# Mixed MLA and forgetting attention, convolution and recurrent blocks on one core: the probabilities of the MLA heads are scaled on GpSimd, with five smaller moves between engines

## The reference, cut to what matters

```python
q = (rms_norm(c_q, g_cq) @ w_uq).reshape(b, l, MLA_HEADS, MLA_QK)
q = rope_tail(rms_norm(q, g_q_mla), cos, sin)
...
s = jnp.einsum('bqhd,bkhd->bhqk', q_blk, k) * scale
s = jnp.where(mask[None, None], s, NEG)
p = jax.nn.softmax(s, axis=-1)
return jnp.einsum('bhqk,bkhd->bqhd', p.astype(v.dtype), v)
```

```python
log_a = LRU_C * r * jax.nn.log_sigmoid(lam)
a = jnp.exp(log_a)
mult = jnp.sqrt(-jnp.expm1(2.0 * log_a))
bterm = mult * (i * xb)
_, hs = lax.associative_scan(_lin_rec_op, (a, bterm), axis=1)
y = hs * g
return y @ w_out
```

## Time and profile before

| | before |
|---|---|
| median of three runs | 1333.24 us (1332.63 to 1337.25) |
| the profiled execution, own time | 1332.28 us |
| its span, first to last instruction | 1330.5 us |
| PE busy | 1302.3 us, 98% |
| DVE busy | 953.9 us, 72% |
| ACT busy | 743.5 us, 56% |
| POOL busy | 342.7 us, 26% |
| mean granted TensorE clock | 0.996 of full speed |

### The profile page before, as it was taken

One profiled execution on the slowest core, in us unless ns is written; L12 is line 12 of the kernel. 1 busy time (PEld: TensorE's weight loads), 2 busy tenths in 40 slices (PEclk: granted clock), 3 DMA queues, 4 the chain that ended last, 5 costly groups with the idle time before them and its releaser, 6 DMA issues. The chain is left out here.

```text
span 1330.5 us, 28216 instructions
## 1 busy us (share of the span) xinstructions
PE 1302.3 (98%) x10550; PEld 1274.0 (96%) x10550; DVE 953.9 (72%) x1426; ACT 743.5 (56%) x1192; POOL 342.7 (26%) x374
## 2 busy tenths in 40 slices
PE   9998999999999999999999999999999989999997
PEld 8987899999999999999899999999999989999996
DVE  6867787655487776655455669998559898999844
ACT  5555554444343554444556556666457886666542
POOL 4632133310011233200006214343103022434311
PEclk9999999999999999999999999999999999999998
DMA  9520155555555455555545545554564445555451
GB/s 307 187 100 1 67 188 190 189 191 180 174 185 188 159 190 189 190 187 177 205 158 186 190 155 199 188 182 147 186 214 173 169 167 198 205 183 180 158 191 55
DMA packets 35370, 230.50 MB, mean 173 GB/s; under 512 B 4062, under 2 KB 5214, under 8 KB 11910
## 3 DMA queue, kind: packets, MB, share of 16 engines
q1 hardware_dynamic: 34228, 226.99, 48.6%
q10 hardware_dynamic: 1058, 2.38, 0.5%
HBM read 228.17 MB, written 1.05 MB: 172 GB/s over the span
## 5 line engine op out<-in xcount | busy, mean ns | idle before, releaser
L392 DVE TENSOR_TENSOR wlo<-raw,whi 128x1024 fp32r<-128x1024 f32 (+1 forms) x446 | 525.5, 1182 | 104.7 <-ACT whi L386 102.2
L427 PE MATMUL ps<-xhi,whi 128*128 128x256 f32 (+2 forms) x1920 | 542.9, 283 | 4.9 <-DVE wlo L392 3.9
L428 PE MATMUL ps<-xlo,whi 128*128 128x256 f32 (+2 forms) x1920 | 542.0, 282 | 0.0
L429 PE MATMUL ps<-xhi,wlo 128*128 128x256 f32 (+2 forms) x1920 | 540.8, 282 | 0.0
L386 ACT ACTIVATE whi<-raw 128x1024 fp32r<-128x1024 f32 (+2 forms) x444 | 446.8, 1011 | 153.3 <-PE ps L429 135.7
L427 PEld LDWEIGHTS ps<-xhi,whi 128*128 128x128 f32 x1920 | 362.4, 189 | 8.6 <-issue 5.6
L429 PEld LDWEIGHTS ps<-xhi,wlo 128*128 128x128 f32 x1920 | 362.9, 189 | 0.0
L428 PEld LDWEIGHTS ps<-xlo,whi 128*128 128x128 f32 x1920 | 360.7, 188 | 0.3
L427 PE MATMUL ps<-hhi,whi 128*128 128x256 f32 (+1 forms) x1184 | 334.3, 282 | 2.0 <-issue 0.8
L429 PE MATMUL ps<-hhi,wlo 128*128 128x256 f32 (+1 forms) x1184 | 333.2, 281 | 0.0
L428 PE MATMUL ps<-hlo,whi 128*128 128x256 f32 (+1 forms) x1184 | 333.0, 281 | 0.0
(11 more groups left out here) (339 smaller groups left out, 1338.1 us busy)
## 6 DMA issues: line engine op xcount, KB each, us to landing
raw<-w SPq DMA_DIRECT2D x182, 1024.0 KB, 4.9
raw<-w SPq DMA_DIRECT2D x40, 768.0 KB, 4.2
raw<-w SPq DMA_DIRECT2D x4, 512.0 KB, 5.4
h<-x_fm ACTq DMA_DIRECT2D x4, 272.0 KB, 5.6
out_fm<-h SPq DMA_DIRECT2D x6, 128.0 KB, 1.9
ws<-ws_src ACTq DMA_DIRECT2D x1, 512.0 KB, 3.5
bs<-bs_rows ACTq DMA_DIRECT2D x1, 512.0 KB, 5.0
consts<-constants SPq DMA_DIRECT2D x1, 508.0 KB, 10.4
```

What stands on the lines that cost most here:

```text
L392: nc.vector.tensor_tensor(wlo[:, w, 0:n], raw[:, slot, col:col + n], whi[:, w, 0:n].bitcast(F32), ALU.subtract).then_inc(wlo_done, 3 if fr ...
L427: nc.tensor.matmul(o, hi, xh, start=start, stop=False)
L428: nc.tensor.matmul(o, hi, xl, start=False, stop=False)
L429: mm = nc.tensor.matmul(o, lo, xh, start=False, stop=stop)
```

## The change

Six edits. (1) The two scalings in `normal` are left to POOL for the eight MLA heads; item 9 and the fox heads stay on DVE, and so does the reciprocal. (2) The power -1/2 of the query sums moves from ACT (Ln, Exp) to DVE, as a shift, a subtraction and two Newton steps, eight instructions of 128x24, in step 7 ahead of the last `k_normed`; the sums themselves are made one step earlier (`q_stats` parts 2 and 3 both in `turn(3)`). (3) `key_spread` stands behind `turn` and `values` of its step in place of ahead of them. (4) Of the log-sigmoid of `lam` only the first two instructions stay where they were; the other 15 move behind `dve_mlp_up` of the first MLP. (5) In mixer B the products of scan and gate for pairs 0, 2 and 4 move from DVE to POOL, and POOL does them before its L2334 and L2337. (6) The rounding of these three products (`B_HIGH`) moves from ACT to DVE, directly ahead of the subtraction.

```diff
@@ -18,6 +18,7 @@
 F32R = mybir.dt.float32r
+I32 = mybir.dt.int32
 ACT = mybir.ActivationFunctionType
@@ -1154,9 +1155,9 @@
                     pe.wait_ge(freed, n)
-                if 1 <= j < 6:
-                    q_stats(j - 1)
-                if j == 6:
+                for part in {1: (0,), 2: (1,), 3: (2, 3), 4: (4,)}.get(j, ()):
+                    q_stats(part)
+                if j == 5:
                     pe.wait_ge(s("q_stats_out"), 2)
@@ -1234,12 +1235,12 @@
                     scores(st)
-                if st in KEY_SPREAD:
-                    key_spread(KEY_SPREAD[st])
                 if st < NIT + 2:
                     turn(st - 2)
                 if items[st - 3][0] == "h":
                     values(items[st - 3][1])
+                if st in KEY_SPREAD:
+                    key_spread(KEY_SPREAD[st])
                 if st >= NIT:
@@ -1458,6 +1459,24 @@
+            def query_power():
+
+                c, y, z, mean = s("q_power"), q_inv[:, :, :], q_neg[:, :, :], q_part[:, 0:3, :]
+                yi = y.bitcast(I32)
+                dve.wait_ge(s("q_mean"), 1)
+                nc.vector.tensor_scalar(yi, mean.bitcast(I32), 1, None, ALU.logical_shift_right).then_inc(c, 1)
+                dve.wait_ge(c, 1)
+                nc.vector.tensor_scalar(yi, yi, -1, 0x5F3759DF, ALU.mult, ALU.add).then_inc(c, 1)
+                for k in range(2):
+                    dve.wait_ge(c, 3 * k + 2)
+                    nc.vector.tensor_tensor(z, y, y, ALU.mult).then_inc(c, 1)
+                    dve.wait_ge(c, 3 * k + 3)
+                    nc.vector.scalar_tensor_tensor(out=z, in0=z, scalar=-0.5, in1=mean, op0=ALU.mult,
+                                                   op1=ALU.mult).then_inc(c, 1)
+                    dve.wait_ge(c, 3 * k + 4)
+                    nc.vector.scalar_tensor_tensor(out=y, in0=z, scalar=1.5, in1=y, op0=ALU.add,
+                                                   op1=ALU.mult).then_inc(c, 1)
+
             def peak(j):
@@ -1485,6 +1504,8 @@
                 nc.vector.reciprocal(sf[:, 3, :], sf[:, 2, :]).then_inc(rc_done, 1)
+                if j > D1:
+                    return
                 dve.wait_ge(rc_done, j + 1)
@@ -1508,6 +1529,8 @@
                     normal(st - 1)
+                if st == 7:
+                    query_power()
                 if st in KEY_FINAL:
@@ -1605,16 +1628,18 @@
             dve.wait_ge(s("params_loaded"), 16)
-            for _ in dve_log_sigmoid(dve, par("lam", 0, NB), half_lam[:, :], tmp[:, 0, 0:NB], tmp[:, 1, 0:NB],
-                            tmp[:, 0, NB:2 * NB], s("lam_step"), s("lam_exp_asked"), s("lam_exp")):
+            lam = dve_log_sigmoid(dve, par("lam", 0, NB), half_lam[:, :], tmp[:, 0, 0:NB], tmp[:, 1, 0:NB],
+                            tmp[:, 0, NB:2 * NB], s("lam_step"), s("lam_exp_asked"), s("lam_exp"))
+            next(lam)
+
+            dve_residual(dve, ph["attn_out"], 1, 1, C1, T1)
+            dve_rstd(dve, 1, C1, T1, ph["mlp0_up"])
+            dve_mlp_up(dve, ph["mlp0_up"], C1, T1)
+            for _ in lam:
                 pass
             nc.vector.tensor_scalar(half_lam[:, :], tmp[:, 0, NB:2 * NB], 4.0, None, ALU.mult).then_inc(s("lam_done"), 1)
             nc.vector.tensor_scalar(par("b_b_a", 0, 2 * NB), par("b_b_a", 0, 2 * NB), 0.5, None,
                                     ALU.mult).then_inc(s("gate_bias_done"), 1)
-
-            dve_residual(dve, ph["attn_out"], 1, 1, C1, T1)
-            dve_rstd(dve, 1, C1, T1, ph["mlp0_up"])
-            dve_mlp_up(dve, ph["mlp0_up"], C1, T1)
             dve_residual(dve, ph["mlp0_down"], 4, 2, C1, T1)
@@ -1714,6 +1739,9 @@
             def low_b(m):
+                if m < 6:
+                    dve.wait_ge(u_done, hid0["b_in"] + m + 2)
+                    nc.vector.tensor_copy(hhi2[:, m:m + 2, :], xb[:, m:m + 2, :]).then_inc(uhi_done, 2)
                 dve.wait_ge(uhi_done, hid0["b_in"] + m + 2)
@@ -1763,8 +1791,9 @@
                                                  ALU.add).then_inc(s("b_scan"), 1)
-                if k in B_MULT:
+                if k in B_MULT and B_MULT[k] >= 6:
                     m = B_MULT[k]
+                    dve.wait_ge(u_done, hid0["b_in"] + m)
                     dve.wait_ge(s("b_scan"), m + 2)
@@ -1828,13 +1857,6 @@
-            def query_power():
-
-                act.wait_ge(s("q_mean"), 1)
-                nc.scalar.activation(q_neg[:, :, :], q_part[:, 0:3, :], ACT.Ln).then_inc(s("q_log"), 1)
-                act.wait_ge(s("q_log"), 1)
-                nc.scalar.activation(q_inv[:, :, :], q_neg[:, :, :], ACT.Exp, scale=-0.5).then_inc(s("q_power"), 1)
-
             def roots(n):
@@ -1902,7 +1924,7 @@
                                          ACT.Copy).then_inc(pt0_done, 1)
-                if j == 5:
+                if j == 4:
                     nc.scalar.activation(q_part[:, :, :], ps[:, 6, 2 * P:2 * P + 4 * HEADS].rearrange(
@@ -1924,8 +1946,6 @@
                     turned(st - 2)
-                if st == 7:
-                    query_power()
                 if st >= 3 and second(st - 3) and items[st - 3][1] < HEADS:
@@ -2109,8 +2129,9 @@
                     nc.scalar.activation(hhi2[:, t, :], xb[:, t, :], ACT.Copy).then_inc(uhi_done, 1)
-                if k in B_HIGH:
+                if k in B_HIGH and B_HIGH[k] >= 6:
                     t = B_HIGH[k]
+                    act.wait_ge(uhi_done, hid0["b_in"] + t)
                     act.wait_ge(u_done, hid0["b_in"] + t + 2)
@@ -2269,7 +2290,7 @@
             c, scale, y, z = q_scale, QK ** -0.5, q_inv[:, :, :], q_neg[:, :, :]
-            pool.wait_ge(s("q_power"), 1)
+            pool.wait_ge(s("q_power"), 8)
             nc.gpsimd.tensor_tensor(z, y, y, ALU.mult).then_inc(c, 1)
@@ -2282,8 +2303,19 @@
             nc.gpsimd.tensor_scalar(z, y, -1.0, None, ALU.mult).then_inc(c, 1)
-            pool.wait_ge(pt0_done, early_turned(D1 + 1))
+            pool.wait_ge(pn_done, parts_done(D1 + 1))
             for i in range(HEADS, NHD):
+                if i % 2 == 0:
+                    if i > HEADS:
+                        pool.wait_ge(d_done, i)
+                    for j in (item_of[i], item_of[i + 1]):
+                        pool.wait_ge(rc_done, j + 1)
+                        for k, (n, a, z) in enumerate(parts(j)):
+                            pr = prob_of(j)[0:n, a:z]
+                            nc.gpsimd.tensor_scalar(pr, pr, soft[0:n, j % 2, 3, k:k + 1], None, ALU.mult).then_inc(pn_done, 1)
+                    pool.wait_ge(pn_done, parts_done(item_of[i + 1] + 1))
+                if i == HEADS:
+                    pool.wait_ge(pt0_done, early_turned(D1 + 1))
                 hd, r = heads[i][4], slice(2 * META * (i % 2), 2 * META * (i % 2) + META)
@@ -2329,6 +2361,11 @@
                                             ALU.subtract).then_inc(ulo_done, 1)
+            for m in (0, 2, 4):
+                pool.wait_ge(s("b_scan"), m + 2)
+                pool.wait_ge(s("b_gelu"), m + 2)
+                nc.gpsimd.tensor_tensor(xb[:, m:m + 2, :], work1[:, m:m + 2, :], h_gates(m, 2),
+                                        ALU.mult).then_inc(u_done, 2)
             for m in (6, 8):
                 pool.wait_ge(s("b_aa"), m + 2)
                 nc.gpsimd.tensor_scalar(square_b(m), square_b(m), 1.0, None, ALU.add).then_inc(s("b_plus"), 1)
```

## The result

| | before | changed |
|---|---|---|
| median | 1332.99 us (6 runs, 1331.82 to 1337.25) | 1339.73 us (6 runs, 1337.98 to 1341.37) |
| ratio, 95% interval | | 1.0046 (1.0034 to 1.0058) |
| the profiled execution, own time | 1332.28 us | 1338.90 us |
| its span | 1330.5 us | 1337.2 us |

The account below looks back on a forecast made before the run. PE, busy 98% of the span, was taken as the bound, so only its holes count. Terms -0.7 + 2.9 - 1.2 + 1.9 = +2.9 us on 1332.28 gave 1335.2; adding 0.96 for the median, 1336 us, range 1330 to 1341.

Parts of the forecast that it names:

- Term A: Attention up to the first MLA head: ACT freed, DVE given eight instructions, PE resumes earlier; -0.7 us, between 0 and -2.1.
- two of its signs: Attention stage: no wait of PE for the keys, and first MLA exponentials about 0.8 us earlier.
- Term B: MLA heads: scaling on POOL is half covered and costs +2.9 us, from 0 to 10.8.
- the ring: MLA heads: maximum, reciprocal, POOL scaling and hand-overs take 2.6 us per head against PE's 2.5; costs 0.9 us in all.
- Term C: Fourth output unit's weight wait: moving `lam` lets the first output tile start earlier; -1.2 us, bounds 0 and -1.86.
- The cover of 3.52 us: Second MLP product: DVE idles 3.52 us before 279.71, so the moved `lam` instructions (3.1 us) cost nothing.
- Term D: Mixer B: POOL's added products delay the root; +1.9 us, middle of 1.0 and 2.7, outer bounds -3.0 and +4.
- the sentence that DVE gains 0.7 us: Mixer B: DVE loses three products of 0.67 us and gains three roundings of about 0.45 us, so -0.7 us.
- Rival R3: New holes between 130 and 148 us drop PE's clock to half speed; 1337 to 1340 us, chance 0.10.
- R1: Attention and mixer B: POOL rarely meets splits, the ring stays hidden; -1 to -5 us, 1327.5 to 1331.5 us, chance 0.18.
- R2: MLA heads: POOL's scaling sets the pace, 1 us more per head; sum +11 us, 1343 us, chance 0.10.
- R4: All edited places: the edits cancel or hide entirely; 1332 to 1334 us, chance 0.07.

Follow-up runs that it names:

- e3: Kernel before with only the 15 `lam` instructions moved behind the first MLP product: 1332.03 us, ratio 0.9992 (0.9982 to 1.0002).
- e7: Kernel before with only the narrow (144-column) scaling of each MLA head on POOL, the wide one on DVE: 1334.10 us, ratio 1.0002.
- e6: Kernel before with mixer B's products on POOL and roundings on DVE, third product behind the four instructions of the root's chain: 1335.53 us, ratio 1.0011.
- e10: Kernel before with only mixer B's three roundings moved to DVE, products staying on DVE: 1335.35 us, ratio 1.0014 (1.0001 to 1.0028).
- e4: Kernel before with only the power -1/2 on DVE and `key_spread` behind the values: 1334.93 us, ratio 1.0012 (1.0001 to 1.0022).
- e1: Kernel before with only the scaling of the eight MLA heads moved to POOL: 1337.87 us, ratio 1.0033 (1.0022 to 1.0043).
- e2: Kernel before with only mixer B's three products on POOL and three roundings on DVE: 1335.35 us, ratio 1.0015 (1.0005 to 1.0025).
- e9: Kernel before with only mixer B's three products on POOL, roundings staying on ACT: 1334.40 us, ratio 1.0012 (0.9999 to 1.0024).

## Why the prediction was right in sign and range, and half the size

Point by point, by its own steps:

- **Term A (edits 2 and 3), -0.7 us: wrong.** No table load is left, and the exponentials of the last fox head came at 121.44, which is 1.2 us earlier when the 1.27 us is taken off that the trace was late by already. But two of its signs did not come: PE waits 1.94 us for the keys, and the first full MLA exponentials came at 128.24 where 126.55 stood, 0.4 us later and not 0.8 earlier, with the 1.27 off. The step that failed is the baseline. The hole that edit 3 closes had, in the profile of before, a stretch of half clock right behind it, and its cost of 1.7 us was in the 123.39. Kernels that have none of edits 1 to 3 up to there and no such stretch (e3, e7) resume at 122.35 and 122.59 us; they were 0.62 and 0.86 us late at 100 us, which leaves 121.7 (e6 and e10 leave the same). The changed kernel has 123.51 - 1.27 = 122.2. So against an undisturbed kernel before it is half a microsecond late, not early. DVE, busy 2.80 of 3 us, was the bound and got 1.7 us more. In the times, with what the clock does behind it, the term is about +1.6 us (e4, 0.1 to 2.9).
- **Term B (scaling on POOL), +2.9 us: right mechanism, somewhat small.** The pass was put at 1.45 us and took 1.58; the ring, the maximum that waits for POOL, the two meetings with a weight split (+0.9 each, 1.2 forecast) are all in the rows. The trace gives 3.5 us, and e1 4.4 (2.9 to 5.7). The upper bound of 10.8 us, by which nothing is covered, was far off. That the length of the ring makes the loss, and not the hand-over, e7 shows.
- **Term C (lam), -1.2 us: right.** -0.92 in the trace, -1.1 by e3. The cover of 3.52 us held.
- **Term D (mixer B), +1.9 us: right size, incomplete reason, and so partly luck.** The last of POOL's four passes ended at 1084.80; with the 4.35 us taken off that is 1080.5, between the 1079.3 and 1081.0 of the forecast, and the loss was 2.3 us. Two entries were too small: a product on POOL took 2.14 us, not 1.62, and a rounding beside POOL 1.51, not 0.45. What failed is the sentence that DVE gains 0.7 us: the roundings were costed alone, and DVE came out about 1.8 us longer (e6). It did not show in the sum, because POOL's chain was as late as DVE's; e6 brought it out. The rule of the Trainium skill (page "SBUF — State Buffer", section "Who interferes with whom") gave 2.7 us for this term by two-input instructions alone; the 2.3 us measured lie halfway between that and the 1.9 said. The same section also names casts and copies among the instructions that can enter a two-port mode, in which VectorE and GpSimd keep each other out for the whole instruction. The 1.51 us of a rounding that takes 0.41 alone agree with that. Had I used it for edit 6, DVE's chain would have come out longer, not shorter.
- **Rival R3 (the clock), 0.10: came true in part.** It was put at new holes between 130 and 148 us; it came at 124 and 1083 us. The first cost about 1.6 us, the second nothing that the traces show. But the kernel before had paid 1.7 us for its own fall at 108 us (term A), so between the two profiles the falls of the attention stage cancel. Its general weight can be read from the runs of the kernel before themselves. They were 102, and sorted by their mean granted clock:

| mean clock | 0.998 | 0.997 | 0.996 | 0.995 | 0.994 | 0.993 |
|---|---|---|---|---|---|---|
| runs | 14 | 15 | 25 | 19 | 21 | 6 |
| mean time, us | 1331.2 | 1331.5 | 1333.1 | 1334.2 | 1335.4 | 1336.4 |

(Two more had 0.992 and 1337.1 us.) A thousandth of clock goes with 1.1 us. The changed kernel's six runs had 0.9935 in the mean, the kernel before 0.9956: 2.3 us of the 6.1 at most, since part of the lower mean is the fall in mixer B, for which the traces show no cost. R1, R2 and R4 did not come.

The sum in the trace: -1.15 + 1.56 + 3.46 - 0.92 + 0.13 + 2.29 = 5.4 us. With the two falls of the clock that cancel taken out (1.7 and 1.6 us) the terms are A +0.5, B +3.5, C -0.9 and D +2.3 where -0.7, +2.9, -1.2 and +1.9 were forecast. All four came out higher, and nearly half of the missing 2.5 us is term A. On top stand 1.3 us that were there ahead of every edit. That part is chance: all twelve other profiles of these experiments are late at the same place, by 0.2 to 1.5 us, so the one profile of before that the forecast stood on was a lucky one.

## What to carry to other kernels

A pass that stands in a ring between engines is priced by the ring's length against the pace of the bound engine, not by how idle the engine is that takes it: POOL was 26% busy and the edit cost 4 us, while the same edit with half of the pass cost nothing that the times show. Before work is moved to POOL, list every instruction of DVE that will run beside it, single-input roundings too; each may get as much longer as the pass of POOL has left to run (a rounding that began 1.23 us ahead of the end of such a pass took 1.1 us longer). Where two chains meet at one wait, find out how late the second one is before mending the first.

## What the runs showed of the hardware that I had not expected

- A rounding of 512 columns to fp32r on DVE took 0.41 us alone and 1.51 us beside a two-input pass of POOL, 3.7 times as long. Two scans of 256 columns went from 1.27 to 2.38 us.
- A single-input scaling of 144 columns on POOL took 0.64 to 0.81 us, and 1.86 us when a weight split of DVE was in front of it.
- TensorE's clock fell to 0.50 in mixer B in all five profiled kernels with the products on POOL, and in none of the nine without, although PE is busy nearly as much there (21.28 of the 25 us from 1070 in e2, 22.49 before). In e2 and e9 the root was already 2.3 and 2.0 us late when it fell, and twice the length (6.8 us, changed kernel) came with the same loss, so no cost of it is seen. Why it falls there the runs leave open.
- The scatter of this kernel's times (1330 to 1339 us over 102 runs of one program) goes with the mean granted clock, about 1.1 us for a thousandth on each of the three chips on which they ran.
